# Attention scores of patterns B and C0 from stacked split operands in a hybrid encoder kernel on one Trainium2 core

## The chip, the cores and the metric

The kernel runs on one core of one Trainium2 chip. The core has a matrix engine (PE, with its weight loads shown apart as PEld), a vector engine (DVE), a scalar engine (ACT), GpSimd (POOL, hardly used here) and DMA queues, of which SP starts most. Times are device microseconds. The metric is the median time of one execution of the whole program, weights read from DRAM included.

## The reference, cut to what matters

Two layers on 512 tokens of width 1024, all in float32. In each layer one input projection feeds four token mixers and four gates; each mixer's output goes through a branch projection, is gated, and the sum goes through an output projection; then a gated MLP with a small convolution.

```python
def differential_attention(...):            # mixer B: 4 heads, 2 maps each
    q = rms_norm(b_q.reshape(b, s, 2, 4, 64), q_norm); k = rms_norm(..., k_norm)
    sc = einsum('bqmhd,bsmhd->bmhqs', q, k) * 64 ** -0.5       # 512 keys for every query
    sc = sc - slopes * |pos_i - pos_j|
    a = softmax(sc); a = a[:, 0] - lam * a[:, 1]
    return einsum('bhqs,bshv->bqhv', a, v)

def dilated_attention(...):                 # mixer C: patterns (128,1), (512,4), (2048,16), 8 heads each
    for j, (window, r) in enumerate(C_PATTERNS):    # C0 is (128, 1): |i - j| <= 64
        o, lse = banded_attention(q_j, k_j, v_j, pos, window // (2 * r), slopes[j])
    return sum_j softmax_j(lse)[j] * o_j
```

Mixer A is a windowed attention with 8 query and 2 key heads, D a latent attention with 8 heads of width 96.

## The kernel before, in words

Every engine runs one instruction stream, without loops: each stream of work is a Python generator that yields a due time in steps, and `together()` merges the streams of an engine in the order of these times. A step is six dense passes of PE (one weight chunk pair on one of four PSUM banks `PJ`). `ORDER` lists the dense blocks with their steps (C0q 0 to 16, C0k 16 to 32, C0v 32 to 48, C1q from 48, ..., Bq 328 to 344, Bk 344 to 360, Bv 360 to 376, br0a 376 to 384, ...; a layer has 752). So the order on each engine is written out beforehand, and an instruction that has to wait holds up everything behind it on its engine.

**Dense products** are done with float32 operands split in two parts: `hi = fp32r(x)` (ACT, L961 for weights) and `lo = x - hi` (DVE, L1481). A product is three fp32r passes, hi.hi + hi.lo + lo.hi (L579). Three weight buffers run ahead of PE by up to 7.6 steps.

**Turns** (`turns()`, L614 on PE): normalised queries and keys lie with tokens on partitions; PE transposes a tile of 128 tokens (four 128x128 transposes) into the single bank `TD`, then ACT takes half of it and DVE the other half to SBUF with a gain (`half_out`: L1180 and L1870 for keys, L1183 and L1873 for queries). The next turn on PE waits until both are done (`td_act`, `td_dve`). Turns of a tensor come every two steps: those of C0's keys at steps 38, 40, 42 and 44, those of B's keys at 366, 368, 370 and 372.

**Attention** runs in the gaps of the dense work. `WINDOW` gives each pattern its steps: C0 49 to 96, A 312 to 376, B 377 to 422, each with 32 units (a query tile of 128 and a head or head and map) in 36 slots. In a slot PE transposes the probabilities of two units ago into `TA`, multiplies those of three units ago with the values, and computes the scores of a new unit into the single bank `S1` (L815, in B L859). DVE adds the position bias and takes the minimum (L2042 for C0 and A, L2023 for B), ACT takes the exponential (L1278, L1366), ACT and DVE copy `TA` to SBUF (L1266 and L1978, L1360 and L2017). In B, DVE also mixes the two maps (L2007 to L2011).

**Scores.** Heads are 64 wide and lie in pairs on the 128 partitions of `kT`. In C0, C1, C2 and B the query operand `q_pad` is a float32 tile with the other head's 64 rows zero; ACT refills it (`pads()`, L1307, L1339). The product of float32 operands appears in the trace as two MATMUL records. In A the scores are already done otherwise: the stationary operand `q_two` has on its 128 rows the high part of the query twice (pass 0), then the low part over zeros (pass 1), the moving operand `kA` has the high part of the key over its low part, and two fp32r passes add up to the product without its lowest term. ACT writes the high part (L1324), DVE copies it to the other rows (L1955) and subtracts to get the low part (L1957); ACT fills the zeros once in a layer (L1320).

**Tables.** `near` holds the position table of A and of C0 (128 x 1280 each), `bias_c12` those of C1 and C2 (128 x 512 each); they are made once, in layer 0 (`setup_rest()`, L1466, L1470, at steps 38 to 45), and are read in both layers.

## Time and profile before

| | |
|---|---|
| median of 3 runs | 2708.42 us (2707.78 to 2709.2) |
| the profiled execution | 2709.8 us, its span 2708.0 us |
| PE busy | 2629.4 us, 97% of the span |
| DVE busy, ACT busy | 1639.1 us (61%), 1231.4 us (45%) |
| granted clock of TensorE, mean | 0.998 |
| DMA | 225.28 MB, mean 83 GB/s |
| copy of x to DRAM, 2048 KB | 11.2 us to landing |

PE's busy time is a union of modelled matmuls: a record of 0.39 us stands for a pass that starts 0.23 us after the one before, so costs are read from the distances between starts. Where the busy time of PE falls short of a stretch, PE waited.

### The profile page before, as it was taken

To read this page: it belongs to the slowest core of one execution; us is meant where nothing else is said; L and a number is where in the kernel's file an instruction comes from. 1 tells how busy PE (TensorE), PEld (TensorE's weight loads), DVE (VectorE), ACT (ScalarE), POOL (GpSimd) and SP (SyncE) were. 2 spreads that over 40 slices of the span, in tenths; PEclk is the share of its full clock that TensorE was granted. 3 is DMA by queue.
4 is the path that set the end of the run, shared out by engine and by line. 5 is a ranking of instruction groups with operands and counts; after the bars stand their busy time and mean duration, and the time that the engine had idled before them with its cause. 6 is when DMAs were issued, how large, how long until landed. Compare 5 with 4: busy or idle time off the path is not lost. (4 is left out here: it accounts for less than half of the span.)

```text
span 2708.0 us, 36172 instructions
## 1 busy us (share of the span) xinstructions
PE 2629.4 (97%) x12982; PEld 2205.3 (81%) x12982; DVE 1639.1 (61%) x3432; ACT 1231.4 (45%) x2514; POOL 1.5 (0%) x6
## 2 busy tenths in 40 slices
PE   7999999999999999999999999999999999999999
PEld 6999987778877778888779998877788777888887
DVE  6554577545666647676664546775356566485665
ACT  5655545444544334333354555544445443443332
POOL 0000000000000000000000000000000000000000
PEclk9999999999999999999999999999999999999999
DMA  5212223222121332332332122221221213333332
GB/s 184 70 55 79 81 65 92 57 77 72 55 78 48 104 100 88 95 103 88 102 117 71 47 87 74 80 86 55 71 78 56 78 47 109 94 94 101 95 100 94
DMA packets 143874, 225.28 MB, mean 83 GB/s; under 512 B 15046, under 2 KB 69458, under 8 KB 142802
## 3 DMA queue, kind: packets, MB, share of 16 engines
q1 hardware_dynamic: 135842, 201.85, 24.8%
q10 hardware_dynamic: 7856, 21.12, 2.1%
q8 instruction: 106, 1.74, 0.3%
q14 instruction: 70, 0.57, 0.1%
HBM read 210.29 MB, written 12.65 MB: 82 GB/s over the span
## 5 line engine op out<-in xcount | busy, mean ns | idle before, releaser
L1481 DVE TENSOR_TENSOR s_wl<-s_raw,s_wh 128x1024 fp32r<-128x1024 f32 (+2 forms) x376 | 453.2, 1206 | 297.9 <-ACT s_wh L961 297.7
L961 ACT ACTIVATE s_wh<-s_raw 128x1024 fp32r<-128x1024 f32 (+2 forms) x376 | 392.0, 1043 | 396.6 <-PE bank L579 298.3
L579 PE MATMUL bank<-s_hTh,s_wh 128*128 128x512 f32 x1216 | 520.9, 428 | 1.6 <-DVE s_work L1839 1.6
L579 PE MATMUL bank<-s_hTh,s_wl 128*128 128x512 f32 x1216 | 474.7, 390 | 0.0
L579 PE MATMUL bank<-s_hTl,s_wh 128*128 128x512 f32 x1216 | 473.9, 390 | 0.0
L579 PE MATMUL bank<-s_wh,s_hTh 128*128 128x512 f32 (+1 forms) x1088 | 458.1, 421 | 4.5 <-DVE s_early L1621 3.4
L579 PE MATMUL bank<-s_wh,s_hTl 128*128 128x512 f32 (+1 forms) x1088 | 426.2, 392 | 0.0
L579 PE MATMUL bank<-s_wl,s_hTh 128*128 128x512 f32 (+1 forms) x1088 | 425.8, 391 | 0.0
L579 PEld LDWEIGHTS bank<-s_hTh,s_wh 128*128 128x128 f32 x1216 | 228.6, 188 | 69.8 <-issue 23.6
L1278 ACT ACTIVATE s_work<-s_work,s_stat 128x128 f32<-128x128 f32 (+3 forms) x320 | 167.5, 524 | 257.5 <-DVE s_work L2053 113.6
L579 PEld LDWEIGHTS bank<-s_hTl,s_wh 128*128 128x128 f32 x1216 | 228.9, 188 | 66.4 <-issue 24.4
L579 PEld LDWEIGHTS bank<-s_wh,s_hTh 128*128 128x128 f32 x1088 | 251.6, 231 | 34.6 <-issue 4.1
L579 PEld LDWEIGHTS bank<-s_wh,s_hTl 128*128 128x128 f32 x1088 | 251.7, 231 | 26.6
L579 PEld LDWEIGHTS bank<-s_wl,s_hTh 128*128 128x128 f32 x1088 | 253.4, 233 | 22.5 <-issue 0.5
L579 PEld LDWEIGHTS bank<-s_hTh,s_wl 128*128 128x128 f32 x1216 | 228.2, 188 | 49.1
L614 PE MATMUL bank<-s_consts,s_work 128*128 128x128 f32 (+1 forms) x1432 | 216.4, 273 | 16.0 <-DVE s_gTl L1878 8.9
L614 PEld LDWEIGHTS bank<-s_consts,s_work 128*128 128x128 f32 (+1 forms) x1432 | 172.6, 139 | 70.7 <-issue 34.3
L1978 DVE COPY s_work<-bank 128x128 f32<-128x128 f32 (+1 forms) x224 | 77.4, 345 | 207.4 <-PE bank L614 98.1
L579 PE MATMUL bank<-s_wh,s_gTh 128*128 128x512 f32 (+1 forms) x432 | 167.4, 387 | 5.6 <-ACT s_work L990 5.2
L579 PE MATMUL bank<-s_wl,s_gTh 128*128 128x512 f32 (+1 forms) x432 | 166.3, 385 | 0.0
L579 PE MATMUL bank<-s_wh,s_gTl 128*128 128x512 f32 (+1 forms) x432 | 166.2, 385 | 0.0
L579 PE MATMUL bank<-s_gTh,s_wh 128*128 128x512 f32 x256 | 111.4, 435 | 5.9 <-DVE s_gTl L1878 3.0
(202 smaller groups left out, 3408.4 us busy)
## 6 DMA issues: line engine op xcount, KB each, us to landing
s_raw<-in_w_in SPq DMA_DIRECT2D x168, 512.0 KB, 3.6
s_raw<-in_ffn_w_up SPq DMA_DIRECT2D x176, 256.0 KB, 3.1
s_raw<-in_ffn_w_down SPq DMA_DIRECT2D x44, 512.0 KB, 3.7
s_raw<-in_w_branch SPq DMA_DIRECT2D x32, 512.0 KB, 3.7
s_raw<-in_w_o SPq DMA_DIRECT2D x16, 512.0 KB, 3.7
x_keep<-s_work ACTq DMA_DIRECT2D x2, 2048.0 KB, 11.2
s_raw<-in_w_in SPq DMA_DIRECT2D x16, 256.0 KB, 3.0
gate_keep<-s_early ACTq DMA_DIRECT2D x4, 1024.0 KB, 4.3
```

Of the source, the lines that this page charges most:

```text
L579: last = mm(PJ[b][:, 0:width], st, mv, start=i == 0 and n == 1, stop=i == ntiles - 1 and n == 3 * chunks)
L614: last = nc.tensor.transpose(dst[0:m, (at + n) * P:(at + n) * P + k], src, ident[0:k, 0:k])
L961: a(wh[:, k % 3, 0:n], raw[:, s, 0:n], ACT.Copy).then_inc(*hi_split.up(own))
L1278: a(probs[:, u % 2, x0:x0 + w], scores[:, u % 2, x0:x0 + w], ACT.Exp, scale=-1.0, bias=stat[:, mins, c:c + 1], accum_out=stat[:, sums, c:c ...
L1481: v.tensor_tensor(wl[:, k % 3, 0:n], raw[:, k % 2, 0:n], wh[:, k % 3, 0:n].bitcast(F32), ALU.subtract).then_inc(*tile_split.up(own))
L1978: v.tensor_copy(probsT[:, u % 2, P * mid:P * hi], src[:, P * mid:P * hi]).then_inc(*ta_dve.up(own))
```

## The change

Scores of C0 and B are computed as those of A are: two fp32r passes with stacked operands.

- Keys: `kC` and `kB` are two tiles each, one for the even and one for the odd head of a pair. Tile `half` has on that head's 64 rows the high part (ACT, with the gain) and on the other 64 rows the low part (DVE). `TD` is read by ACT for both halves (2 instructions of 64 x 512), and after that by DVE for both (2 of 64 x 512); before, each took one instruction of 128 x 256.
- Queries: `q_near` (C0) and `q_four` (B). ACT writes the high part in eight pieces of two instructions (64 x 256), as many as it wrote into `q_pad` before; DVE follows each with a copy to the other rows and a subtraction (new generators `stacks_c()` and `stacks_b()`). ACT fills zeros with 2 instructions for C0 and 4 for B in a layer.
- Place: `kB[1]` lies over the second half of `near` (C0's table) and part of `bias_c12`. ACT starts two DMAs that copy these tables to DRAM after C2 in layer 0, and two that bring them back after B in layer 0. ACT waits for the first two before it writes `kB[1]` in layer 0; DVE waits for the last two before C0 in layer 1.
- `q_pad` stays for C1 and C2. Dense blocks, windows and due times of everything else stay.

```diff
-PADS = dict(C0=16, C1=8, C2=8, B=16)
+PADS = dict(C1=8, C2=8)
+STACKS = dict(C0=0, A=16, B=32)
...
+    kC = [stacked[:, at:at + 2048].rearrange("p (c n) -> p c n", c=4) for at in (AD + 2048, AD + 12288)]
+    q_near = stacked[:, AD + 10240:AD + 12288].rearrange("p (c h s n) -> p c h s n", c=4, h=2, s=2)
+    kB = [t.rearrange("p (c n) -> p c n", c=4) for t in (stacked[:, AD + 2048:AD + 4096], tables[:, NEAR:NEAR + 2048])]
+    q_four = [t.rearrange("p (c h s n) -> p c h s n", c=2, h=2, s=2) for t in (stacked[:, 6144:7168], stacked[:, AD + 14336:AD + 15360])]
@@ PE: attention(), attention_b() @@
-                        if name == "A":
-                            pe.wait_ge(*q_stacked.at(l, pads_of(name, step)))
+                        if name in STACKS:
+                            pe.wait_ge(*q_stacked.at(l, STACKS[name] + pads_of(name, step)))
...
-                        pe.wait_ge(*q_padded.at(l, n_pad[0] + pads_of("B", step)))
+                        pe.wait_ge(*q_stacked.at(l, STACKS["B"] + pads_of("B", step)))
...
+                def near_scores(u, out):
+                    lo, hi, _mid = near_keys(u)
+                    h = u % 8
+                    return [(out[:, P * lo:P * hi], q_near[:, h // 2, h % 2, part, :],
+                             kC[h % 2][:, h // 2, P * lo:P * hi], part == 0, part == 1) for part in range(2)]
...
                 def b_scores(u, out):
                     n = 4 * (u % 2) + (u % 8) // 2
-                    return [(out[:], q_pad[:, n // 2, n % 2, :], kT[:, n // 2, :], True, True)]
+                    c = n // 2
+                    return [(out[:], q_four[c % 2][:, c // 2, n % 2, part, :], kB[n % 2][:, c, :], part == 0, part == 1) for part in range(2)]
@@ ACT: turns(), keys of B (those of C0 likewise, at END["C0k"] + 6.4 + 2 * t) @@
-                yield from k_out(END["Bk"] + 6, kT, "bk")
+                for t in range(4):
+                    yield END["Bk"] + 6.4 + 2 * t
+                    src = group()
+                    for half in range(2):
+                        mine = slice(64 * half, 64 * half + 64)
+                        if l == 0 and t == 0 and half == 1:
+                            act.wait_ge(tables_moved, 16 * 2)
+                        act.wait_ge(*own.done(l))
+                        a(kB[half][mine, :, P * t:P * t + P], src[mine, :].rearrange("p (c n) -> p c n", c=4), ACT.Copy,
+                          scale=prm[mine, ROW["bk"]:ROW["bk"] + 1]).then_inc(*(td_act if half else act_step).up(own))
@@ ACT: pads(), pieces of B (those of C0 at slot[0][1] - 6 + 1.5 * piece for the first two) @@
+                def stacks_of_b():
+                    first, slot = done, slots("B")
+                    for piece in range(8):
+                        t, g = piece // 2, piece % 2
+                        yield slot[4 * piece - 4][1] + 0.8 * slot[0][2] if piece >= 2 else slot[0][1] - 6 + 3 * piece
+                        if piece == 0:
+                            act.wait_ge(*td_dve.at(l, B_HEADS - 4))
+                            act.wait_ge(*sq_used.at(l, sq_used.each))
+                        if piece:
+                            act.wait_ge(*s_ready.at(l, first + 4 * piece - 4 if piece >= 2 else first))
+                        if piece < 2:
+                            for half in range(2):
+                                other = slice(64 - 64 * half, 128 - 64 * half)
+                                act.wait_ge(*own.done(l))
+                                a(q_four[g][other, :, half, 1, :], q_pad[other, 0:2, half, :], ACT.Copy).then_inc(*q_zeroed.up(own))
+                        for half in range(2):
+                            mine = slice(64 * half, 64 * half + 64)
+                            act.wait_ge(*own.done(l))
+                            a(q_four[g][mine, :, half, 0, :], qT[mine, g:4:2, P * t:P * t + P], ACT.Copy).then_inc(*q_hi.up(own))
@@ ACT: attentions(), layer 0, after C2 @@
+                    act.wait_ge(*s_biased.at(l, 48))
+                    act.dma_start(near_keep, near[:, 1, :]).then_inc(tables_moved, 16)
+                    act.dma_start(bias_keep, bias_c12[:]).then_inc(tables_moved, 16)
@@ ACT: after B, layer 0: the same two back @@
@@ DVE: turns(), keys of B (those of C0 likewise, at END["C0k"] + 6.8 + 2 * t) @@
-                yield from k_out(END["Bk"] + 6, kT, "bk")
+                for t in range(4):
+                    yield END["Bk"] + 6.8 + 2 * t
+                    src = group()
+                    for half in range(2):
+                        mine, other = slice(64 * half, 64 * half + 64), slice(64 - 64 * half, 128 - 64 * half)
+                        dve.wait_ge(*own.done(l))
+                        v.scalar_tensor_tensor(kB[half][other, :, P * t:P * t + P], src[mine, :].rearrange("p (c n) -> p c n", c=4), prm[mine, ROW["bk"]:ROW["bk"] + 1],
+                                               kB[half][mine, :, P * t:P * t + P].bitcast(F32), ALU.mult, ALU.subtract).then_inc(*(td_dve if half else dve_step).up(own))
@@ DVE: pieces of B (those of C0 in stacks_c(), with q_near), 0.3 steps after ACT's @@
+            def stacks_b():
...
+                    for half in range(2):
+                        n += 1
+                        mine, other = slice(64 * half, 64 * half + 64), slice(64 - 64 * half, 128 - 64 * half)
+                        dve.wait_ge(*q_hi.at(l, n))
+                        dve.wait_ge(*own.done(l))
+                        v.tensor_copy(q_four[g][other, :, half, 0, :], q_four[g][mine, :, half, 0, :].bitcast(F32)).then_inc(*dve_step.up(own))
+                        dve.wait_ge(*own.done(l))
+                        v.tensor_tensor(q_four[g][mine, :, half, 1, :], qT[mine, g:4:2, P * t:P * t + P],
+                                        q_four[g][mine, :, half, 0, :].bitcast(F32), ALU.subtract).then_inc(*q_stacked.up(own))
@@ DVE: attentions() @@
+                if l:
+                    yield WINDOW["C0"][0]
+                    dve.wait_ge(tables_moved, 16 * 4)
```

## Rows read from the trace of the kernel before

**Rows 1.** The page, busy time of each engine (us, share, instructions).
```profile
PE 2629.4 (97%) x12982; PEld 2205.3 (81%) x12982; DVE 1639.1 (61%) x3432; ACT 1231.4 (45%) x2514; POOL 1.5 (0%) x6
```
**Rows 2.** Busy time by stretch, layer 0's windows of C0 and B (stretch, its length, busy).
```profile
96.10:208.00 111.90, 111.85 (x606) 106.02 (x606) 57.24 (x164) 59.73 (x152) 0.00 (x0) 1.00 0.18 53
782.70:888.00 105.30, 102.28 (x469) 73.68 (x468) 66.86 (x154) 46.24 (x102) 0.00 (x0) 1.00 0.18 51
```
**Rows 3.** Groups of PE by form: the float32 score products (count, busy us, mean ns).
```profile
L859 PE MATMUL bank<-s_work,s_q_pad 128*128 128x512 f32 x128 | 66.4, 600 | 3.4 <-DVE s_stat L2023 3.1
L815 PE MATMUL bank<-s_work,s_q_pad 128*128 128x384 f32 x64 | 27.7, 515 | 0.0
L815 PE MATMUL bank<-s_work,s_q_pad 128*128 128x256 f32 x64 | 20.6, 404 | 0.0
```
**Rows 4.** Timeline of PE around a score unit of B (start, length).
```profile
782.46 0.40 PE L579 MATMUL bank<-s_gTh,s_wl 128*128 128x512 f32 x1
782.70 1.02 PE L859 MATMUL bank<-s_work,s_q_pad 128*128 128x512 f32 x2
...
783.79 0.40 PE L579 MATMUL bank<-s_gTl,s_wh 128*128 128x512 f32 x1
```
**Rows 5.** Timeline of PE around units of C0, 256 and 384 keys.
```profile
97.86 0.39 PE L579 MATMUL bank<-s_wh,s_hTl 128*128 128x512 f32 x1
...
98.77 0.40 PE L579 MATMUL bank<-s_wl,s_hTh 128*128 128x512 f32 x1
...
120.82 0.86 PE L815 MATMUL bank<-s_work,s_q_pad 128*128 128x384 f32 x2
...
121.75 0.40 PE L579 MATMUL bank<-s_wl,s_hTh 128*128 128x512 f32 x1
```
**Rows 6.** Timeline of PE around stacked units of A, 256 and 384 keys.
```profile
641.71 0.39 PE L579 MATMUL bank<-s_gTh,s_wl 128*128 128x512 f32 x1
641.94 0.40 PE L815 MATMUL bank<-s_stacked 128*128 128x256 f32 x2
...
642.17 0.40 PE L579 MATMUL bank<-s_gTh,s_wh 128*128 128x512 f32 x1
...
682.28 0.60 PE L815 MATMUL bank<-s_stacked 128*128 128x384 f32 x2
682.72 0.39 PE L579 MATMUL bank<-s_wh,s_hTh 128*128 128x512 f32 x1
```
**Rows 7.** Groups of ACT and DVE whose forms are nearest to the new instructions.
```profile
L1189 ACT ACTIVATE s_gTh<-bank,s_gain 128x512 fp32r<-128x512 f32 x8 | 5.5, 689 | 17.9 <-PE bank L614 17.9
L1878 DVE SCALAR_TENSOR_TENSOR s_gTl<-bank,s_gain,s_gTh 128x512 fp32r<-128x512 f32 x8 | 6.0, 751 | 7.2 <-ACT s_gTh L1189 6.9
L1957 DVE TENSOR_TENSOR s_stacked<-s_work,s_stacked 64x256 fp32r<-64x256 f32 x32 | 13.4, 419 | 1.1
L1955 DVE CAST s_stacked<-s_stacked 64x256 fp32r<-64x256 f32 x32 | 9.3, 289 | 10.4 <-ACT s_stacked L1324 7.7
```
**Rows 8.** Timeline of the second turn of C0's keys, layer 0, on three engines.
```profile
82.22 0.60 PE L614 MATMUL bank<-s_consts,s_work 128*128 128x128 f32 x4
...
82.85 0.48 ACT L1180 ACTIVATE s_work<-bank,s_prm 128x256 f32<-128x256 f32 x1 [0.66 <-PE bank L614]
...
83.43 0.48 DVE L1870 TENSOR_SCALAR s_work<-bank,s_prm 128x256 f32<-128x256 f32 x1 [1.64 <-ACT s_work L1180]
```
**Rows 9.** Timeline around the turns of B's keys, layer 0 (DVE first, then PE).
```profile
763.47 0.48 DVE L1870 TENSOR_SCALAR s_work<-bank,s_prm 128x256 f32<-128x256 f32 x1 [1.22 <-ACT s_work L1180]
...
765.00 0.82 PE L614 MATMUL bank<-s_consts,s_work 128*128 128x128 f32 x6
...
768.88 0.82 PE L614 MATMUL bank<-s_consts,s_work 128*128 128x128 f32 x6
```
**Rows 10.** Busy time by stretch in A's window; the granted clock is the number before the last two.
```profile
660.00:662.50 2.50, 1.14 (x8) 1.06 (x9) 1.98 (x5) 0.45 (x2) 0.00 (x0) 0.97 0.00 0
662.50:665.00 2.50, 2.50 (x8) 2.02 (x7) 0.71 (x3) 1.28 (x6) 0.00 (x0) 0.50 0.72 210
```

More of the change, by code:

```diff
@@ L251, in _build @@
     wh, wl = sb("wh", [P, 3, HALF], F32R), sb("wl", [P, 3, HALF], F32R)
-    near = sb("near", [P, 2, NEAR])
+    with nc.sbuf_tensor("s_tables", [P, 2 * NEAR + 2 * SEQ], F32R) as tables:
+        pass
+    near, bias_c12 = sb("near", [P, 2, NEAR]), sb("bias_c12", [P, 2, SEQ])
     bias_b = sb("bias_b", [P, TT, SEQ])
-    bias_c12 = sb("bias_c12", [P, 2, SEQ])
     AD = 7168
@@ L390, in _build @@
     pad_clear = sem("pad_clear")
+    tables_moved = sem("tables_moved")
     nc.disable_value_cache = True
@@ L1347, in pads @@
                 done += WINDOW["A"][2]
-                yield from tiles_of("B", qT, B_HEADS, by_map)
+                yield from stacks_of_b()
             def attention_b():
@@ L1896, in turns @@
                     yield from q_out(END[f"C{j}q"] + 6, CQ[j], 8 + 4 * j)
-                    yield from k_out(END[f"C{j}k"] + 6, CK[j], "ckn")
+                    if j:
+                        yield from k_out(END[f"C{j}k"] + 6, CK[j], "ckn")
+                        continue
+                    for t in range(4):
+                        yield END["C0k"] + 6.8 + 2 * t
+                        src = group()
+                        for half in range(2):
+                            mine, other = slice(64 * half, 64 * half + 64), slice(64 - 64 * half, 128 - 64 * half)
+                            dve.wait_ge(*own.done(l))
+                            v.scalar_tensor_tensor(kC[half][other, :, P * t:P * t + P], src[mine, :].rearrange("p (c n) -> p c n", c=4), prm[mine, ROW["ckn"]:ROW["ckn"] + 1],
+                                                   kC[half][mine, :, P * t:P * t + P].bitcast(F32), ALU.mult, ALU.subtract).then_inc(*(td_dve if half else dve_step).up(own))
                 for t in range(4):
@@ L1942, in turns, with stacks_c @@
                     lo_out(gTl[:, 0:4, cols], gTh[:, 0:4, cols], group(), td_dve, gain[:, 20:21])
+            def stacks_c():
+                slot, n = slots("C0"), STACKS["C0"]
+                for piece in range(8):
+                    t, g = piece // 2, piece % 2
+                    yield (slot[4 * piece - 4][1] + 0.8 * slot[0][2] if piece >= 2 else slot[0][1] - 6 + 1.5 * piece) + 0.3
+                    for half in range(2):
+                        n += 1
+                        mine, other = slice(64 * half, 64 * half + 64), slice(64 - 64 * half, 128 - 64 * half)
+                        dve.wait_ge(*q_hi.at(l, n))
+                        dve.wait_ge(*own.done(l))
+                        v.tensor_copy(q_near[other, 2 * g:2 * g + 2, half, 0, :], q_near[mine, 2 * g:2 * g + 2, half, 0, :].bitcast(F32)).then_inc(*dve_step.up(own))
+                        dve.wait_ge(*own.done(l))
+                        v.tensor_tensor(q_near[mine, 2 * g:2 * g + 2, half, 1, :], qT[mine, 2 * g:2 * g + 2, P * t:P * t + P],
+                                        q_near[mine, 2 * g:2 * g + 2, half, 0, :].bitcast(F32), ALU.subtract).then_inc(*q_stacked.up(own))
             def stacks():
-                slot, n = slots("A"), 0
+                slot, n = slots("A"), STACKS["A"]
                 for piece in range(8):
@@ L2084, in attentions @@
                 yield from attention_b()
-            return norm1(), dense(), turns(), stacks(), attentions(), c_combine()
+            return norm1(), dense(), turns(), stacks_c(), stacks(), stacks_b(), attentions(), c_combine()
         together(setup_first(), setup_rest(), splits(), *[shifted(stream, TOTAL * l) for l in range(DEPTH) for stream in layer(l)])
```

75 lines of the change are left out of this document (48 added, 27 removed).

## The prediction

> **What bounds the kernel now.** I read the page first: PE is busy 97% of the span, DVE 61%, ACT 45% [rows 1]. The sum is therefore made on PE: time that leaves PE's stream leaves the span, as long as nothing makes PE wait in its place. Next I read the busy time by stretch for the two windows that change [rows 2]: in C0's window PE waits 0.05 us of 111.9, with DVE busy 57.2 us (51%); in B's it waits 3.0 us of 105.3, with DVE busy 66.9 us (64%). Layer 1 repeats both within 0.3 us. So PE is the bound in both, and in B's window DVE's work, which comes in bursts, already shows a little. Then I took the costs of single units from PE's timeline, and last the chain PE, ACT, DVE of a turn, because it is the one place where the change lengthens something that PE waits for directly.
>
> **The score products (what is removed from PE).** The page's durations overlap, so I use distances between starts. Dense passes start 0.23 us apart. In B, from the dense pass at 782.46 to the second one after the unit (783.79) there are 1.33 us; two dense distances go off, and the float32 unit costs 0.87 us [rows 4]. The new unit is two fp32r passes of 512 columns, the same form as two dense passes: 0.46 us. That saves 0.41 us; with the small products that often stand before a unit some of the second pass's weight load may show, so I take 0.40.
> For 256 keys the old unit is 98.77 - 97.86 - 0.46 = 0.45 us [rows 5], and A's stacked one 642.17 - 641.94 = 0.23 us [rows 6]: saves 0.22, taken 0.21. For 384 keys, both read behind small products: old 121.75 - 120.82 - 0.23 = 0.70 us [rows 5], stacked 682.72 - 682.28 = 0.44 us [rows 6]: saves 0.26; by the columns (midway between 0.22 and 0.41) it would be 0.31; taken 0.28.
> Counts: a float32 unit has two records, so there are 64 units of B, 32 with 384 keys and 32 with 256 [rows 3]. The sum is 64 x 0.40 + 32 x 0.28 + 32 x 0.21 = 25.6 + 9.0 + 6.7 = 41.3 us off PE (bounds 38 and 44).
> The Trainium skill ("TensorE: Matmul & The Clock Gate", Back-to-back issue gap) puts a lone pass of 512 columns at some 216 ns start to start. The trace has 0.23 us here; by the page's figure B would give 2 us more, as an estimate. The trace decides.
>
> **Keys: two instructions for one on each of ACT and DVE, in series.** Today a turn of C0's keys goes: PE starts the transposes at 82.22, ACT starts at 82.85 and takes 0.48, DVE starts at 83.43 and takes 0.48 [rows 8]; TD is free 1.7 us after PE began. Turns are two steps apart: 12 x 0.23 + some 0.45 for the transposes = 3.2 us. New: each of ACT and DVE has two instructions of 512 columns per partition. Nearest rows: ACT 0.69 with a gain from PSUM to fp32r, DVE 0.75 for the same multiply and subtract [rows 7]. I take the full duration for 64 partitions, since time goes with the columns. With about 0.05 between dependent instructions of one engine and 0.1 between engines: 0.63 + 1.43 + 0.1 + 1.55 + 0.1 = 3.8 us until PE may begin the next turn, against 3.2. PE stalls 0.6 us at each of three following turns, 1.8 us in layer 1. In layer 0 DVE also has the tables to make between these turns (ten additions of 256 to 512 columns, at 0.4 to 0.7 us by the forms of [rows 7]); by the third turn it is 1 us late: 2.9 us. Together 4.7 us (from 0, if ACT and DVE turn out faster on half the partitions, to 8). The pieces of q_near (1.5 us of DVE each, below) fall before the fourth turn's DVE part; that turn has 7 us until C0's first unit, which hides it.
>
> **B's keys**, in A's window. Here DVE is through with the first turn at 763.95, and PE turns again at 765.00 [rows 9]: 1.05 us in hand. New, ACT and DVE together add 0.96 + 1.07 = 2.0 us: PE waits about 1.0. Behind DVE's part stand the copy of TA and the bias of A's next unit, behind these the exponential, and behind that ACT's part of the next turn: all of it 2 us later, so that the turn due at 768.88 [rows 9] holds PE again, by some 1.6 us. The fourth turn comes as long after the third as the third after the second (3.9 us), now with no unit beside it: no stall. But DVE then has the key parts, a weight split and two pieces of q_four (1.5 us each) before A's last tile is normalised and split, and for that tile PE must wait at its turn and before br0a: 1.2 us. In all 3.8 us a layer, 7.6 us (from 0 to 12).
>
> **Queries.** ACT's 16 small copies per pattern and layer stay, only their target changes: nothing. Added on ACT are six zero fills a layer, under 0.7 us each (ACT's 512-column form) [rows 7], before the windows, where ACT is under 60% busy: nothing. Added on DVE per pattern and layer: 16 x (0.29 + 0.42) = 11.3 us [rows 7]. Each piece is due three slots (8 us) before PE needs it, so PE does not wait for the pieces themselves; they cost by standing before other DVE work. In C0's window DVE goes to (57.2 + 11.3) / (111.9 - 7.9) = 66%: I give 0.5 us a layer, 1 us (0 to 4). In B's window it goes to (66.9 + 11.3) / (105.3 - 12.8) = 85%, and higher where a branch product is taken in (two DVE instructions of 512 columns, 1.4 us by [rows 7], in a step that PE now passes sooner). PE's waits there were 3.0 us a layer; I expect them to about double: 2.5 us a layer, 5 us (0 to 14, were most of the added DVE time on the path).
>
> **Tables.** Four DMAs of 0.5 to 0.7 MB on ACT's queue, issued where ACT has slack. The first two have 190 steps until ACT waits for them, behind which B's second key half would stand; the last two have 379 steps until DVE waits before C0 of layer 1, where everything of DVE stands behind. The engines' DMA share is 0.18 in B's window [rows 2]. Nothing (0 to 1).
>
> **Clock.** In A's window PE was busy only 1.14 of 2.5 us, and in the next 2.5 us the granted clock was 0.50, that is 1.2 GHz [rows 10]. There PE does 1.25 us of work in 2.5. One more such event, with its tail, for new stalls close together: 2 us (0 to 10). The Trainium skill (same page, A second HAM failure mode) warns that PE's frequent short idle gaps can make the clock swing between its two levels. By that rule each of my new stall places would cost such a stretch too; the trace has it after one of its places of short waits [rows 10], and not in B's window, where the granted clock stayed 1.00 with 3.0 us of waits [rows 2].
>
> **Sum.** 41.3 - 4.7 - 7.6 - 1 - 5 - 2 = 21.0 us. Made on the profiled execution, whose own time is 2709.8 us (span 2708.0), that is 2688.8; it lay 1.4 us above the median of 2708.42, so I predict 2687.4, given as 2687 us.
>
> **Rivals.**
> 1. *The whole gain arrives.* Half-width instructions run faster than their rows, or waits of PE in other places absorb the new ones. For it: PE waits almost never in C0's window now, and DVE and ACT idle half of it. Against it: 1.05 us in hand at 763.95 is read from the trace. Time: 2709.8 - 1.4 - 41 + 4 (small stalls) = 2671 us.
> 2. *DVE becomes the bound in B's window and around the key turns.* At 85% of an in-order stream with bursts, most of the added 22.6 us in the two B windows would lie on the path, beside 12 us at B's keys and 8 at C0's: the 41 us are used up. For it: 85%. Against it: pieces have 8 us of room. Time: about 2706 us.
> 3. *The clock swings.* With some ten new stall places, each followed by a stretch as in rows 10 at 1.2 GHz (about 1.6 us lost), 16 us go instead of 2: 2701 us.
> 4. *Slower than before*, one mechanism: the key turns hold DVE's splits of the weights so long that PE waits for weights. DVE makes one weight part of 1024 columns every four steps, up to 7.6 steps ahead (46 passes at 0.23 us, 10 us). If the key turns and pieces made DVE more than 10 us late, every further microsecond would be PE's, in four places; 10 us each over that limit gives back all and more: about 2716 us. It decides from a lag of some 20 us, and the added DVE work around a key turn is 4.3 + 3 us. So it is unlikely.
> 5. That the change does not do what it says: two passes of 512 columns costing more than 0.46 is excluded by the dense passes, which have the form.
>
> **How the numbers follow.** Forecast 0.52, rival 1 0.22, rival 2 0.10, rival 3 0.09, rival 4 and unknown mishaps 0.07. The range takes in the forecast's own bounds and reaches to rival 1 and rival 3: 2669 to 2703 us. A change within 0.2% (5.4 us) of 2708.4 can't be told from none. Faster by more means under 2703: 0.52 + 0.22 + 0.09, and part of rival 2, together 0.87; the same 0.07; slower 0.06.
>
> **What would show it.** After the change, B's units should stand in PE's timeline as two records whose cost is 0.46 us, C0's at 0.23 and 0.34 to 0.44. B's window should be some 10 us shorter (about 95 us), C0's 7 to 8 us. In the chain waits, PE's turns should show new waits for DVE's key parts, 0.6 us apiece at C0 and 1 to 1.6 us at B. DVE's share in B's window should be near 85%, and PE's idle time there near 5.5 us a layer. Wrong would be the prediction's middle part if PE's waits at the key turns are absent (then rival 1), or if B's window shrinks by less than 5 us (rival 2); and if the granted clock shows more than five or six half-speed stretches, rival 3.

## The result and the profile after

| | before | after |
|---|---|---|
| median of 4 runs on one chip | 2708.63 us (2707.78 to 2709.2) | 2729.62 us (2728.64 to 2731.34) |
| ratio | | 1.0079 (95%: 1.0066 to 1.0091) |
| span of the profiled execution | 2708.0 us | 2729.5 us |
| granted clock of TensorE, mean | 0.998 | 0.994 |

The change makes the kernel 21 us slower; I had forecast 21 us faster. The page of the kernel after, against [rows 1]: PE does less work and is still busy for nearly as long, while DVE has 62.9 us more.

```profile
PE 2612.9 (96%) x12982; PEld 2205.5 (81%) x12982; DVE 1702.0 (62%) x3576; ACT 1253.7 (46%) x2542; POOL 1.5 (0%) x6
```

**Where the time went.** I cut both traces at the same steps of PE's stream. Busy time by stretch, layer 0: C0's key turns (steps 32 to 49), C0's window (49 to 96), B's key turns (360 to 377), B's window (377 to 424). Columns: stretch and length, busy PE, PEld, DVE, ACT, POOL, granted clock, DMA share, GB/s. Before:

```profile
69.70:94.80 25.10, 25.10 (x119) 21.04 (x118) 18.51 (x39) 16.11 (x28) 0.00 (x0) 1.00 0.34 102
94.80:210.10 115.30, 115.25 (x620) 109.18 (x620) 58.86 (x164) 61.47 (x156) 0.00 (x0) 1.00 0.19 52
745.90:781.60 35.70, 32.93 (x184) 27.73 (x183) 22.40 (x56) 18.51 (x48) 0.00 (x0) 1.00 0.31 101
781.60:900.60 119.00, 115.98 (x539) 85.23 (x538) 74.64 (x168) 52.00 (x113) 0.00 (x0) 1.00 0.20 56
```

After, the same steps:

```profile
70.10:98.10 28.00, 25.67 (x120) 20.87 (x119) 23.69 (x48) 22.51 (x38) 0.00 (x0) 1.00 0.24 72
98.10:215.70 117.60, 112.66 (x620) 107.42 (x620) 69.41 (x192) 59.65 (x152) 0.00 (x0) 0.99 0.20 56
751.20:793.30 42.10, 34.46 (x183) 28.25 (x182) 29.95 (x68) 25.18 (x57) 0.00 (x0) 0.97 0.27 87
793.30:912.40 119.10, 107.77 (x540) 86.21 (x539) 82.88 (x191) 51.42 (x111) 0.00 (x0) 0.98 0.19 56
```

The differences are +2.9, +2.3, +6.4 and +0.1 us; layer 1 gives +2.2, +1.0, +6.6 and +0.4. Together they are 21.9 us, and the spans differ by 21.5, so the rest of the program takes as long as before. B's window is the telling one: its score products became 12.8 us shorter, and its length is the same.

**What PE waited for.** Waits of PE in B's window (us in total, times, longest), first before:

```profile
PE bank L859 <- DVE s_stat L2023: 1.6, 2, 0.8
PE bank L850 <- DVE s_work L2032: 0.7, 1, 0.7
PE bank L850 <- DVE s_work L2017: 0.5, 2, 0.3
```

and after:

```profile
PE bank L861 <- DVE s_work L2125: 6.7, 6, 1.4
PE bank L870 <- DVE s_stat L2131: 1.9, 2, 0.9
PE bank L861 <- DVE s_work L2140: 1.4, 1, 1.4
PE bank L625 <- DVE s_work L2119: 1.0, 2, 0.7
```

L861 (before L850) are B's products with the values, L2125 (before L2017) is DVE's copy of half of the transposed probabilities: this wait grew from 0.5 to 6.7 us, the whole list from 2.8 to 11.0. One such wait in the timeline of the kernel after (start, duration, engine, line):

```profile
810.01 0.29 DVE L2063 CAST s_stacked<-s_stacked 64x256 fp32r<-64x256 f32 x1
810.33 0.42 DVE L2065 TENSOR_TENSOR s_stacked<-s_work,s_stacked 64x256 fp32r<-64x256 f32 x1
...
810.85 0.29 DVE L2063 CAST s_stacked<-s_stacked 64x256 fp32r<-64x256 f32 x1
811.17 0.42 DVE L2065 TENSOR_TENSOR s_stacked<-s_work,s_stacked 64x256 fp32r<-64x256 f32 x1
811.63 0.42 DVE L2125 COPY s_work<-bank 128x256 f32<-128x256 f32 x1
812.08 0.69 DVE L1680 SCALAR_TENSOR_TENSOR s_work<-s_work,bank 128x512 f32<-128x512 f32 x1
812.17 0.86 PEld L861 LDWEIGHTS bank<-s_work 128*128 128x128 f32 x7 [1.79 <-issue]
812.20 0.91 PE L861 MATMUL bank<-s_work 128*128 128x128 f32 x6 [1.39 <-DVE s_work L2125]
```

A whole piece of `q_four`, four instructions in 1.6 us, stands just ahead of the copy, and PE is idle for 1.39 us. The piece is early for its own reader and late for its neighbour.

**The clock.** After such waits come stretches at half speed. Busy time by stretch around this one:

```profile
807.50:810.00 2.50, 1.93 (x10) 1.51 (x11) 2.37 (x5) 1.26 (x4) 0.00 (x0) 1.00 0.35 134
810.00:812.50 2.50, 1.11 (x7) 0.67 (x6) 2.26 (x6) 0.77 (x2) 0.00 (x0) 1.00 0.00 0
812.50:815.00 2.50, 1.57 (x11) 1.30 (x10) 2.43 (x6) 0.86 (x3) 0.00 (x0) 0.95 0.00 0
815.00:817.50 2.50, 2.50 (x8) 1.84 (x7) 2.33 (x7) 1.02 (x2) 0.00 (x0) 0.50 0.00 0
```

PE was busy 4.6 of 7.5 us, then the granted clock was 0.50, that is 1.2 GHz. At B's keys the same happens, and PE's timeline shows the price:

```profile
790.51 0.47 PE L590 MATMUL bank<-s_gTh,s_wh 128*128 128x512 f32 x1 [1.93 <-DVE s_gTl L1937]
...
793.34 0.63 PE L590 MATMUL bank<-s_gTl,s_wh 128*128 128x512 f32 x1
793.76 0.63 PE L590 MATMUL bank<-s_gTh,s_wl 128*128 128x512 f32 x1
...
794.92 0.62 PE L870 MATMUL bank<-s_stacked 128*128 128x512 f32 x2
795.38 0.39 PE L590 MATMUL bank<-s_gTh,s_wh 128*128 128x512 f32 x1
795.62 0.40 PE L590 MATMUL bank<-s_gTl,s_wh 128*128 128x512 f32 x1
```

Passes stand 0.42 us apart in place of 0.23, some eight of them: about 1.6 us lost. Before the program's end there are 3 such stretches in the kernel before and 10 in the kernel after, six of these in the four stages of the table (both layers).

### The profile page after: what moved, and what is told of

It is laid out like the page before. It is cut to its first block and busy times, and to the rows that moved or that the text cites. A ratio compares the mean times of both kernels' runs of the same rounds, so it can differ in the third digit from the quotient of the medians.

```text
span 2729.5 us, 36446 instructions
## 1 busy us (share of the span) xinstructions
PE 2612.9 (96%) x12982; PEld 2205.5 (81%) x12982; DVE 1702.0 (62%) x3576; ACT 1253.7 (46%) x2542; POOL 1.5 (0%) x6
## 5 line engine op out<-in xcount | busy, mean ns | idle before, releaser
L1540 DVE TENSOR_TENSOR s_wl<-s_raw,s_wh 128x1024 fp32r<-128x1024 f32 (+2 forms) x376 | 453.2, 1207 | 289.1 <-ACT s_wh L973 288.6
L590 PE MATMUL bank<-s_hTh,s_wh 128*128 128x512 f32 x1216 | 504.9, 415 | 1.5 <-DVE s_work L1898 1.5
L590 PE MATMUL bank<-s_wh,s_hTh 128*128 128x512 f32 (+1 forms) x1088 | 448.6, 412 | 5.0 <-DVE s_early L1680 3.3
L1309 ACT ACTIVATE s_work<-s_work,s_stat 128x128 f32<-128x128 f32 (+3 forms) x320 | 167.4, 524 | 262.6 <-DVE s_work L2161 113.5
L1297 ACT ACTIVATE s_work<-bank 128x256 f32<-128x256 f32 (+1 forms) x224 | 78.2, 349 | 85.8 <-PE bank L625 84.5
```

Of the source, the lines that this page charges most:

```text
L590: last = mm(PJ[b][:, 0:width], st, mv, start=i == 0 and n == 1, stop=i == ntiles - 1 and n == 3 * chunks)
L1297: a(probsT[:, u % 2, P * lo:P * mid], src[:, P * lo:P * mid], ACT.Copy).then_inc(*ta_act.up(own))
L1309: a(probs[:, u % 2, x0:x0 + w], scores[:, u % 2, x0:x0 + w], ACT.Exp, scale=-1.0, bias=stat[:, mins, c:c + 1], accum_out=stat[:, sums, c:c ...
L1540: v.tensor_tensor(wl[:, k % 3, 0:n], raw[:, k % 2, 0:n], wh[:, k % 3, 0:n].bitcast(F32), ALU.subtract).then_inc(*tile_split.up(own))
```

## The experiments

"Work" below is the sum of the distances between the ends of successive PE passes, each taken at the median of its form; what is longer by over 0.15 us is a "wait"; it is taken from one profiled execution of each kernel. In B's window of layer 0 the kernel before has 113.5 us of work and 5.1 of waits; the kernel after 100.7 of work, 16.0 of waits and 1.7 from half speed. All were timed against the kernel before on the same chip (its medians there: 2707.86 for the first four, 2708.09 for the second, 2708.38 for the third, 2708.25 for the last). Where a time is compared with the kernel after (2729.62 us), the two were not run at the same time: the medians of the kernel before beside them differ by up to 0.8 us. The diffs are shortened, and most waits and increments of semaphores are left out of them.

**One pattern at a time.** `b_only` changes B, with its tables, and leaves C0 as it was; `c_only` is the reverse.

```diff
 # b_only
-PADS = dict(C1=8, C2=8)
-STACKS = dict(C0=0, A=16, B=32)
+PADS = dict(C0=16, C1=8, C2=8)
+STACKS = dict(A=0, B=16)
 # c_only
+PADS = dict(C1=8, C2=8, B=16)
+STACKS = dict(C0=0, A=16)
```

> Only B's scores are stacked; C0 stays on float32 operands with half_out turns. Reading the two traces against each other step by step gives C0's part of the change about +5.3 us in layer 0 and +3 us in layer 1. If the parts are independent: 2729.6 - 8 = 2721 us, B's window as in the full change. Rival (the loss is the moved tables and their DMAs, which stay here): no different from this. Rival (the two patterns disturb each other): nearer to 2710 or to 2730.

> Only C0's scores are stacked; B stays on float32 operands, the tables are not moved to DRAM. If the parts are independent: 2708.6 + 8 = 2717 us, with PE's waits in C0's window near 5 us a layer. If the loss came with B or with the table DMAs alone: 2700 us or less.

Measured, as expected for `b_only` and 4 us better than expected for `c_only`: `b_only` 2721.04 us (ratio 1.0048, 1.0033 to 1.0063), `c_only` 2713.35 us (1.0020, 1.0010 to 1.0031). The losses add: 13.2 + 5.5 = 18.7 of 21 us. B's stages in `b_only` repeat those of the full change (B's keys 42.2 us, B's window 119.5), and so do C0's keys in `c_only` (28.0). C0's window does so but for one thing: it takes 116.0 us in place of 117.6, with the same 7.2 us of waits, because the stretch at half speed that the full change has there is absent; in layer 1 it is the same (115.2 us against 116.5). Two such stretches, some 3 us, cover the 2 us that the sum lacks. So the parts are independent except for the clock, and both lose, B more.

**Are the pieces or the shorter units to blame?** `narrow` keeps everything of the change, but DVE's two instructions for pieces 2 to 7 write 2 of 128 columns (most of the low and doubled parts are left out). `dummy` is the kernel before, float32 products and all, to which DVE's instructions for these pieces are added, into tiles that nothing reads.

```diff
 # narrow (q_near likewise)
+w = P if piece < 2 else 2
-v.tensor_copy(q_four[g][other, :, half, 0, :], q_four[g][mine, :, half, 0, :].bitcast(F32))
+v.tensor_copy(q_four[g][other, :, half, 0, 0:w], q_four[g][mine, :, half, 0, 0:w].bitcast(F32))
 # dummy, on the kernel before
+yield slot[4 * piece - 4][1] + 0.8 * slot[0][2] + 0.3
+v.tensor_copy(dst(g)[other, :, half, 0, :], qT[mine, cols(g), P * t:P * t + P])
+q = qT[mine, cols(g), P * t:P * t + P]
+v.tensor_tensor(dst(g)[mine, :, half, 1, :], q, q, ALU.subtract)
```

> The full change, but in pieces 2 to 7 of C0 and of B DVE copies and subtracts only 2 of 128 columns of each head (the low and doubled query parts of three of four query tiles are left out), so 48 instructions a layer of 0.29 or 0.42 us shrink to some 0.1. Theory (DVE's pieces, due just before the copy of TA, make PE wait and cost clock events): PE's idle time in C0's window falls from 5 to under 1 us and in B's from 11 to some 4 us, half-speed stretches from 10 to about 4, time 2693 us (2685 to 2702). Rival (the shorter score units alone expose the chain scores, bias, exponential, transposes): 2720 us or more, with the waits in place.

> The kernel before, float32 scores, plus DVE's pieces 2 to 7 of C0 and B as in the change (same forms, same due times, same waits on ACT's query pieces), written to tiles nobody reads. Theory (the pieces cost by themselves, through their place in DVE's order): PE begins to wait for the copy of TA in both windows, some 8 to 15 us in all, 2717 to 2724 us. Rival (only the combination with PE's shorter units costs): 2708 to 2712 us.

Measured: `narrow` 2714.18 us (1.0023, 1.0014 to 1.0033), `dummy` 2725.13 us (1.0064, 1.0049 to 1.0079). B's window in `narrow`, then in `dummy`:

```profile
787.80:902.40 114.60, 106.48 (x539) 84.93 (x538) 78.24 (x191) 51.27 (x110) 0.00 (x0) 1.00 0.20 59
```

```profile
783.40:907.70 124.30, 118.33 (x540) 86.10 (x539) 83.62 (x192) 52.20 (x113) 0.00 (x0) 0.99 0.19 54
```

The pieces alone, without any gain, make B's window 5.3 us longer (about 4 us of waits and a stretch at half speed) and C0's 3.5 (118.8 against 115.3). That is twice 8.8 us, which accounts for the 17 us of `dummy`. I had given them 3 us a layer. The shorter products show when `dummy` is set beside the kernel after, which has the same pieces: in B's window work falls by 12.8 us, and waits rise from about 9 to 16.0. So over half of what the products save there is eaten by waits that were hidden behind longer products. Both causes are real.

`narrow` came out between what its theory (2693 us) and its rival (2720 us) said: it still waits 13.2 us in B's window, against 5.1 before, and has 7 stretches at half speed, where I expected about 4. But it does not take the pieces away. DVE's instructions for them in B's window (count, busy us, mean ns, idle before), in the kernel after and in `narrow`:

```profile
L2063 DVE CAST s_stacked<-s_stacked 64x256 fp32r<-64x256 f32 x12 | 3.5, 289 | 5.3 <-ACT s_stacked L1391 4.4
L2065 DVE TENSOR_TENSOR s_stacked<-s_work,s_stacked 64x256 fp32r<-64x256 f32 x12 | 5.0, 419 | 0.4
```

```profile
L2065 DVE CAST s_stacked<-s_stacked 64x4 fp32r<-64x4 f32 x12 | 2.0, 164 | 5.3 <-ACT s_stacked L1391 4.4
L2067 DVE TENSOR_TENSOR s_stacked<-s_work,s_stacked 64x4 fp32r<-64x4 f32 x12 | 1.9, 157 | 0.4
```

Cut to 2 columns they still take 3.9 of 8.5 us, and DVE still stands idle for 5.3 us in front of them, mostly until ACT has written its part of the piece. How the 8.1 us of additional waits in `narrow` divide between the shorter products and what is left of the pieces was therefore not measured.

**Place of the pieces.** `moved` puts the two halves of a piece into two different slots, each behind the position bias and no longer just ahead of the copy of `TA`.

```diff
 # due times for piece >= 2
-yield slot[4 * piece - 4][1] + 0.8 * slot[0][2] + 0.3
 for half in range(2):
+    yield slot[4 * piece - 3 + half][1] + 0.3 * slot[0][2]
```

> The full change, with DVE's query pieces 2 to 7 of C0 and B due elsewhere: each half piece alone, right after the position bias of a slot, one and two slots later, instead of both halves (1.5 us) right before the copy of TA. Same instructions. Theory that place is what costs about the pieces: the waits in B's window fall from 16 us a layer to the 13 of the run with the narrow pieces, in C0's from 7 to 5, fewer half-speed stretches: 2719 us (2714 to 2723). Rival that only DVE's total load counts: 2727 to 2731 us.

Measured: 2726.19 us (1.0065, 1.0050 to 1.0080), 3.4 us less than the kernel after and nearer to the rival than to the theory. C0's window is 1.7 us shorter, mainly because a stretch at half speed is absent; B's 0.9. The waits in B's window stay (16.6 us), although DVE's idle time in front of the pieces falls there from 5.3 to 1.2 us: the place decides which copy is late, not how much is late.

**Key turns.** `khi` lets DVE's lower half follow ACT's lower half at once (an own semaphore), in place of waiting for both.

```diff
-.then_inc(*(td_act if half else act_step).up(own))
+.then_inc(*(td_act if half else k_hi).up(own))
 # DVE
-src = group()                      # waits for both halves of ACT
+dve.wait_ge(*(td_act.at(l, n_turn[0]) if half else k_hi.at(l, 4 + t + 1)))
```

> The full change, but DVE's part of the first key half waits only for ACT's part of that half, so the two engines overlap in a key turn. The chain of a turn falls from 3.8 to 3.1 us, under the 3.2 us between C0's turns. Theory (the series of four instructions is what holds PE at the key turns): the stage of C0's keys, +2.9 and +2.1 us against before, falls to under +1 in each layer, that of B's keys from +5.4 to +3.5 or less; together 6 us: 2723 us. Rival (the turns wait for DVE's other work, not for the series): 2728 us or more.

Measured: 2721.52 us (1.0047, 1.0032 to 1.0062), 8.1 us less than the kernel after. C0's key stage goes from 28.0 to 26.7 us, B's from 42.1 to 39.9; I had expected about 2 us of each. So the longer series of instructions in a turn does cost PE time, and over a third of what the two key stages lost (3.5 of 9.3 us) was avoidable.

**Branch products.** For each gate's branch product DVE has two instructions of 0.69 us in a row (L1680, in the timeline above, and L1683). `late` moves the second one by some slots, in the kernel after; `before_late` does the same in the kernel before.

```diff
-if g is not None:
+if g is not None and name not in ("br0a", "br0b"):
+def late_adds():
+    for cb, k in ((0, 7), (1, 26)):
+        for m in range(4):
+            yield slots("B")[k + m][1] + 0.3 * slots("B")[0][2]
+            v.tensor_tensor(merged[:, 4 * cb + m, :], merged[:, 4 * cb + m, :], GATES[m], ALU.add)
```

> The full change, with the eight additions of a layer into the merged sum of branch products br0a and br0b (0.69 us each on DVE) taken out of the bursts and put one to a slot behind the position bias, a few steps later. Theory (in B's window the shorter units meet DVE's bursts: PE waits where branch products and B's chain fall together): the waits of B's window fall from 16 to 10 or 12 us a layer, 2718 to 2722 us. Rival (the chain of a unit, bias, exponential, mixing, transposes, is too long for the shorter slot wherever it stands): 2727 us or more.

> The kernel before with the same eight additions moved. If the bursts cost it, too: its 5 us of waits a layer in B's window fall to 3, 2704 us. If its longer units cover the bursts: no change, 2708 us.

Measured: `late` 2723.14 us (1.0053, 1.0036 to 1.0070), 6.5 us less than the kernel after, just short of what was expected: its waits in B's window are 14.0 us, not 10 to 12, and the stretch at half speed there is gone. `before_late` 2703.57 us (0.9984, 0.9975 to 0.9994), which beats the kernel before by 4.5 us (0.16%) and is the fastest complete kernel here. B's window in `before_late`:

```profile
782.40:899.40 117.00, 115.52 (x539) 85.32 (x538) 74.40 (x168) 52.07 (x113) 0.00 (x0) 1.00 0.20 57
```

Its DVE work is the same as before, 2.0 us less of length. Waits fall from 5.1 to 3.1 us, as expected. Spreading this burst paid even where DVE is busy 63%.

**All mendings together, and C0 alone with them.** `all4` is `late` + `khi` + `moved`, and ACT writes the doubled high part of each piece in place of DVE's copy. `c_all4` is `c_only` with the same four.

```diff
 # all4, q_four (q_near likewise); DVE's tensor_copy is gone
-a(q_four[g][mine, :, half, 0, :], qT[mine, g:4:2, P * t:P * t + P], ACT.Copy).then_inc(*q_hi.up(own))
+a(q_four[g][mine, :, half, 0, :], qT[mine, g:4:2, P * t:P * t + P], ACT.Copy).then_inc(*act_step.up(own))
+act.wait_ge(*own.done(l))
+a(q_four[g][other, :, half, 0, :], qT[mine, g:4:2, P * t:P * t + P], ACT.Copy).then_inc(*q_hi.up(own))
```

> The changed kernel with four things put right at once: piece halves in separate slots (as in moved), DVE's two halves of a key turn let loose one after the other (as in khi), the gates' second instruction taken out of the branch products' steps (as in late), and the doubled high part of each piece written by ACT instead of DVE (16 instructions of 0.29 us per pattern and layer off DVE). If PE's waits come from separate bursts on DVE, the three measured gains add: 2729.6 - 3.4 - 8.1 - 6.5 = 2711.6 us, and ACT's copies give 2 to 4 us more: 2708 us. If the waits come from one stream being too full, each gain takes part of the same waits and the clock keeps eight to ten half-speed stretches: 2713 to 2718 us.

> Only C0 stacked (as in c_only: B's scores stay float32, no tables moved), with the four mendings of all4 on C0's part. c_only was at 2713.35 us. Mending by bursts: C0's key turns give 2.4 us, pieces in separate slots 2 to 3, ACT's copies 1 to 2, the gates' instruction 4.5 (as in before_late): 2713.4 - 10.5 = about 2703 us, level with before_late (2703.6). If C0's window still keeps 5 us of waits a layer, 2705 to 2708 us.

Measured: `all4` 2725.21 us (1.0057, 1.0041 to 1.0074) and `c_all4` 2713.17 us (1.0016, 1.0006 to 1.0025). They miss the 2708 and 2703 us expected by 17 and 10 us, and lie outside what I had allowed for gains that share waits. C0's key stage in `all4` is at 27.9 us again: what `khi` had won is gone. `c_all4` has 6 stretches at half speed where `c_only` has 2. So I took ACT's copies back.

> The changed kernel with the halves of a key turn overlapped (khi) and the gates' second instruction moved (late), nothing else. If both gains stand by themselves: 2729.6 - 8.1 - 6.5 = 2715.0 us. If all4's 2725 showed that the gains do not add: 2720 us or more.

> all4 without ACT's copies of the high part. all4's stages show that the key turns lost what khi had gained there (C0's keys +2.8 us against +1.6). If ACT's copies spoiled it by standing on ACT before the key parts, this kernel is at 2712 to 2716 us; if the mendings do not add whoever makes the copies, 2720 to 2725 us.

Measured: `khi_late` 2716.03 us (1.0028, 1.0017 to 1.0040), `moved_khi_late` 2713.79 us (1.0022, 1.0012 to 1.0031). Without ACT's copies the gains do add (to within 1 and 2 us). C0's key turns and B's window, first in `moved_khi_late`, then in `all4`:

```profile
70.10:96.80 26.70, 25.21 (x119) 20.79 (x118) 23.57 (x48) 22.42 (x37) 0.00 (x0) 1.00 0.25 76
...
789.80:905.50 115.70, 107.30 (x539) 85.70 (x538) 82.23 (x191) 51.18 (x110) 0.00 (x0) 0.99 0.20 57
```

```profile
69.90:97.80 27.90, 25.62 (x120) 20.88 (x119) 24.62 (x47) 23.75 (x42) 0.00 (x0) 1.00 0.24 73
...
789.60:908.10 118.50, 107.61 (x539) 86.42 (x538) 79.04 (x179) 55.58 (x122) 0.00 (x0) 0.98 0.20 57
```

Taking 3.2 us off DVE and giving 4.4 us to ACT, which is busy 47%, made B's window 2.8 us longer. For C0's keys the traces show why. All of PE's waits in that stage, in `moved_khi_late` and then in `all4`:

```profile
PE bank L626 <- DVE s_stacked L1976: 1.5, 1, 1.5
```

```profile
PE bank L626 <- DVE s_stacked L1982: 1.5, 1, 1.5
PE bank L591 <- ACT s_work L1010: 0.8, 1, 0.8
```

The turn waits as before; the new wait is for L1010, ACT's copy of a finished dense product out of its bank, which ACT starts at 95.19 in place of 93.60 because the doubled copies of two pieces stand ahead of it. In layer 1 the same wait is 2.4 us against 0.6. For B's window the cause was not separated.

**What holds PE with short units.** On `narrow`, two cuts: `late`'s move, and B's mix of the two probability maps in 2 of 512 columns from the third pair on (most of the mix is left out). `before_mix` makes that cut alone in the kernel before.

```diff
 # narrow_mix, narrow_both, before_mix; narrow_late and narrow_both have late's move
+w = SEQ if u < 4 else 2
-v.scalar_tensor_tensor(mixed[:, u // 2 % 2, :], p1, share, p0, ALU.mult, ALU.add)
+v.scalar_tensor_tensor(mixed[:, u // 2 % 2, 0:w], p1[:, 0:w], share, p0[:, 0:w], ALU.mult, ALU.add)
```

> The kernel narrow (pieces 2 to 7 written in 2 columns of 128) with the gates' second instruction out of the branch products' steps. narrow still had 13.2 us of waits in B's window against 5.1 before. If these are waits for DVE's bursts, the branch products' DVE part is one: 13.2 falls to some 9 and the time to about 2708 us. If they come from the chain score, bias, exponential, mix, copy being too long for a shorter step, 13.2 loses only the 2 us that before_late lost, and the time is 2710 us or more.

> The kernel narrow with B's mix of two probability maps also cut to 2 of 512 columns from the third pair of each layer on: some 0.6 us less of DVE per pair, in the middle of the chain between B's exponential and its transposes. If B's waits with short units come from DVE having no room left in a step, PE's waits in B's window fall from 13.2 to 5 to 7 us a layer, and the time from 2714 to about 2700 us. If they come from the chain score product, bias, next score product alone (S1 is one bank), the mix does not matter: 12 to 13 us of waits and 2713 us.

> narrow with both cuts: the gates' second instruction out of the branch products' steps, and B's mix in 2 of 512 columns from the third pair of a layer on. In B's window narrow had 13.2 us of waits, with the first cut 10.4, with the second 9.4. If all of it is DVE having too little room in the shorter step, the cuts add: 13.2 - 2.8 - 3.8 = 6.6 us, near the 5.1 of before, and the time is about 2702 us. If a latency that no DVE work makes (score, bias, exponential in series) holds the rest, the second cut gives little on top of the first: 9 to 10 us of waits and 2706 us or more.

> The kernel before with B's mix cut to 2 of 512 columns from the third pair of a layer on. With the long float32 units DVE has room in a step: B's waits fall from 5.1 by at most 2 us a layer, 2705 to 2708 us; so most of the 3.8 us a layer that the same cut gave with short units is what the short units made of DVE's load. If the cut gives 3.8 us here too, DVE's load was as much on the path before: 2701 us.

| | median us, ratio (95%) | B's window, layer 0: length, waits |
|---|---|---|
| before | | 119.0, 5.1 |
| before_mix | 2706.73, 0.9993 (0.9983 to 1.0002) | 117.9, 4.1 |
| before_late | 2703.57, 0.9984 (0.9975 to 0.9994) | 117.0, 3.1 |
| narrow | 2714.18, 1.0023 (1.0014 to 1.0033) | 114.6, 13.2 |
| narrow_late | 2707.91, 0.9995 (0.9985 to 1.0004) | 111.7, 10.4 |
| narrow_mix | 2708.18, 0.9996 (0.9986 to 1.0005) | 110.5, 9.4 |
| narrow_both | 2702.60, 0.9978 (0.9969 to 0.9988) | 109.1, 7.5 |

The same cut of the mix takes 1.0 us of waits with long products and 3.8 with short ones, and the two cuts nearly add (6.6 forecast, 7.5 measured). `narrow_late` and `before_mix` came out as expected; `narrow_mix` lies midway between its two forecasts (2700 and 2713 us). So with shorter products, and what is left of the pieces beside them, DVE's work turns into waits, work which before had room. It is not the whole: with both cuts 7.5 us are left, while 5.1 less 2.0 and 1.0 would be left with long products. Some 5 us a layer therefore are not removed by these cuts; whether they are the latency of score, bias, exponential and mix in series, or what `narrow` leaves of the pieces (3.9 us of DVE and some 6 us of its idle time, in `narrow_both` as well), was not separated.

## Why the prediction was wrong, step by step

Both layers together, in us (loss positive), measured in the profiled execution:

| term | forecast | measured |
|---|---|---|
| B's score products | -25.6 | -25.7 |
| C0's score products | -15.7 | -10.0 |
| C0's key turns | 4.7 | 5.1 |
| B's key turns | 7.6 | about 10.7 |
| waits in C0's window | 1 | 10.5 |
| waits in B's window | 5 | 22.2 |
| clock | 2 | about 8.6 |
| sum | -21.0 | 21.4 |

The distances between passes give the measured column: at B's keys waits went from 3.2 to 8.5 us (layer 1 to 8.6), in C0's window from 1.3 and 1.7 to 7.2 and 6.3, in B's from 5.1 and 5.2 to 16.0 and 16.5. Half-speed passes cost 2 x (1.4 + 1.7) in the windows, and 2.4 us is what B's key stages lost beside their waits. These waits are more than the profile's list of waits shows, because the list starts when PE's modelled end of the pass before is over.

- **Score products of B: right.** 0.46 us for a unit (794.92 to 795.38 above), as worked out from the dense passes [rows 4]; over the 64 units the median saved is 0.39 us, forecast 0.40.
- **Score products of C0: the size was off by a third.** Timelines of PE in the kernel after, around a unit of 256 keys and one of 384:

```profile
104.07 0.48 PE L826 MATMUL bank<-s_stacked 128*128 128x256 f32 x2
104.39 0.51 PE L590 MATMUL bank<-s_wh,s_hTh 128*128 128x512 f32 x1
104.74 0.40 PE L590 MATMUL bank<-s_wl,s_hTh 128*128 128x512 f32 x1
...
121.59 0.60 PE L826 MATMUL bank<-s_stacked 128*128 128x384 f32 x2
122.03 0.45 PE L590 MATMUL bank<-s_wh,s_hTh 128*128 128x512 f32 x1
122.32 0.40 PE L590 MATMUL bank<-s_wl,s_hTh 128*128 128x512 f32 x1
```

  With 384 keys the unit and the next dense pass take 122.32 - 121.59 = 0.73 us, against 0.93 before [rows 5]: saved 0.20, not 0.28. With 256 keys more is lost. From the end of the pass before a unit to the end of the second dense pass behind it, the medians over 32 units are 0.97 us before and 0.88 after with 256 keys, so that 0.09 is saved and not 0.21; with 384 keys they are 1.17 and 0.93. The cost is in the dense pass after the unit: its successor starts 0.29 (384 keys) or 0.35 us later (256 keys), not 0.23. I had read A's stacked units [rows 6] only up to that pass's start, and the one of 256 keys behind a dense pass, where it takes 0.23 us, while most of C0's stand behind small products and take 0.32 (104.07 to 104.39). The Trainium skill ("TensorE: Matmul & The Clock Gate", Back-to-back issue gap) says that in a stream of weight loads and matmuls both set the spacing; the trace agrees in that the delay shows behind passes of 256 and 384 columns and not behind B's of 512 (795.38 to 795.62). With -15.7 corrected to -10.0 the sum would still have been a gain of 15 us.
- **C0's key turns: right** (4.7 against 5.1), stage by stage. **B's key turns: the mechanism was right.** The two turns wait as worked out (first two lines; the third is the turn of A's last tile):

```profile
771.31 0.85 PE L625 MATMUL bank<-s_consts,s_work 128*128 128x128 f32 x6 [0.91 <-DVE s_tables L2000]
776.99 0.85 PE L625 MATMUL bank<-s_consts,s_work 128*128 128x128 f32 x6 [1.62 <-DVE s_tables L2000]
787.93 0.66 PE L625 MATMUL bank<-s_consts,s_work 128*128 128x128 f32 x4 [1.88 <-DVE s_work L2183]
```

  Forecast 1.0 and 1.6, measured 0.91 and 1.62. The third term, A's last tile, I put at 1.2; PE waits 1.88 for the tile and 1.93 for its split (790.51 above), where it waited 1.5 before: 2.3 more, nearly double the term. Half-width instructions cost the full duration, as assumed from [rows 7]. Groups of instructions of DVE and ACT at B's keys (count, busy us, mean ns, idle before):

```profile
L2000 DVE SCALAR_TENSOR_TENSOR s_tables<-bank,s_prm,s_tables 64x512 fp32r<-64x512 f32 x4 | 3.0, 756 | 0.1
...
L1273 ACT ACTIVATE s_tables<-bank,s_prm 64x512 fp32r<-64x512 f32 x4 | 2.7, 684 | 0.2
```

- **Waits in the two windows: the step that failed.** I had 0.5 and 2.5 us a layer; it was 5 and 11. The step reads "Each piece is due three slots (8 us) before PE needs it, so PE does not wait for the pieces themselves", which was true, and then prices what stands behind them from DVE's share of time. The share is no measure of it: DVE is busy 82.9 of 119.1 us, 70% after 63% before and far from the 85% of the forecast, and the waits tripled. What moved is what comes just before a copy that PE needs within one slot, while that slot lost 0.41 us of PE work. I also took the 3.0 us of idle in [rows 2] as the size of the exposed part. And I counted the pieces by their durations alone: DVE also stands idle for 5.3 us a window in front of them. `dummy`, and the kernel after set beside it, show that both halves of the step were too small, what the pieces cost and what the shorter products expose: about 4 and 7 us of waits a layer in B's window. My bounds of 4 us for C0's and 14 us for B's windows were both exceeded.
- **Clock: rival 3's mechanism.** 7 more stretches at half speed, where I had one more. It comes on top of the waits and does not replace them. The Trainium skill's warning (same page, A second HAM failure mode) that frequent short idle gaps make the clock swing, which I gave 0.09, holds here in kind: [rows 10] were no exception. It does not hold for every stall: the 11 waits listed above for B's window came with one stretch.
- **Tables: nothing, as forecast.** No wait for `tables_moved` shows, and the four stages account for the whole difference of the spans (21.9 of 21.5 us). No run has B's stacked scores without the tables, so what their transfers may cost inside B's stages was not measured.
- **Rivals.** The whole gain (rival 1) is excluded by the turns. Rival 2 named the right place but kept the sum at zero. Rival 4 ended on the right side with the wrong mechanism: PE waits for a weight part (L1540) once, 1.4 us, after 0.9 before (L1481). The true outcome is rivals 2 and 3 at once, which I had not allowed to come together; each alone stayed under 2708.

## What to carry to other kernels

Where an in-order engine alternates with PE at every step, shortening PE's part of the step does not only save time: it also shortens what hid the other engine's burst. A way to price such a change, which no run here tested as a forecast, is the slack of the tightest handshake in the step (here the copy of the transposed probabilities) less the longest burst that can stand before it; the engine's share of time misled. Work that has eight microseconds to spare for its own reader can still hold up its neighbours. Spreading bursts helped in `late` and `before_late` (2 us of waits a layer each), but halving and moving the pieces (`moved`) did not lower the waits in B's window, so it must be measured case by case. A cheap test comes before anything else is built: add the new instructions to the old kernel with nobody reading them. Here that alone gave 17 us of loss.

## What the runs showed of the hardware

- ACT and DVE instructions of 64 partitions by 512 columns take as long as with 128 partitions (0.68 and 0.75 us here, 0.69 and 0.75 in [rows 7]): a tile split by partitions into two instructions takes twice as long.
- A dense pass that follows two short passes (256 or 384 columns) starts its successor 0.35 or 0.29 us later in place of 0.23.
- At 1.2 GHz passes of 512 columns stand 0.42 us apart, and a stretch costs 1.6 us. PE had been idle before each of the six in the four stages: several times close together (as between 807.5 and 815), twice for 1.9 us (up to 787.9 and 790.5), but in C0's window (the stretch that begins at 186.7 us, and its like in layer 1) only once, for 1.4 us. In B's window idle times of 1.0 and 1.4 us (up to 853.5 and 861.8) brought none, and neither did those of at most 0.8 us in the kernel before. So it does not come out of these runs which wait brings a stretch.
